# Gate and up projections of an encoder layer: one of the seven Strassen products is itself split by a second Strassen level

## The reference

```python
x = x + 0.5 * swiglu(rmsnorm(x, norm_ffn1), w_ffn1_gate, w_ffn1_up, w_ffn1_down)
x = x + hybrid_mixer(rmsnorm(x, norm_mix), ...)
x = x + 0.5 * swiglu(rmsnorm(x, norm_ffn2), w_ffn2_gate, w_ffn2_up, w_ffn2_down)
y = rmsnorm(x, norm_final)

def swiglu(h, w_gate, w_up, w_down):        # D_FF = 2816
    return (jax.nn.silu(h @ w_gate) * (h @ w_up)) @ w_down
```

## Time and profile before

| | |
|---|---|
| median of 3 runs (lowest to highest) | 2169.91 us (2168.96 to 2171.39) |
| profiled execution, first to last instruction (its span) | 2169.4 us; no time of its own outside the span is listed |
| PE busy | 2138.6 us (99%), 11956 matmuls |
| DVE, ACT, POOL busy | 69%, 39%, 15% |
| moved by DMA | 301.17 MB, 139 GB/s over the span |
| gate and up stages | 34 to 575 us and 1359 to 1900 us of the span |

### The profile page before, as it was taken

How to read it: one execution, slowest core, us unless ns; L and a number is a source line. 1 busy time by engine, 2 the same in 40 slices (tenths; PEclk the granted TensorE clock), 3 DMA queues, 4 the chain that set the end, 5 groups by cost and what they waited for, 6 DMA issues and landing times.

```text
span 2169.4 us, 32769 instructions
## 1 busy us (share of the span) xinstructions
PE 2138.6 (99%) x11956; PEld 1921.3 (89%) x11956; DVE 1499.5 (69%) x2704; ACT 842.6 (39%) x1688; POOL 330.1 (15%) x324
## 2 busy tenths in 40 slices
PE   6999999999999999999999999999999999999998
PEld 6999999999988888888888888899999999988887
DVE  7766677676666686988754556777777667757676
ACT  7333222222343355755543334422323322333343
POOL 7111111111100002201002344211111111100000
PEclk9999999999999999999999999999999999999999
DMA  4322222332586566433355972222322222387554
GB/s 128 101 82 91 92 88 88 97 101 97 176 292 211 174 208 171 126 111 94 94 149 170 292 229 101 65 94 92 115 82 82 92 91 88 113 291 257 174 186 166
DMA packets 245987, 301.17 MB, mean 139 GB/s; under 512 B 24194, under 2 KB 159746, under 8 KB 245828
## 3 DMA queue, kind: packets, MB, share of 16 engines
q1 hardware_dynamic: 237188, 285.97, 41.2%
q10 hardware_dynamic: 8640, 13.11, 1.7%
HBM read 206.29 MB, written 88.47 MB: 136 GB/s over the span
## 4 chain that ended last, share of the span: by engine, by line
PE 95%; DVE 2%; POOL 1%; DMA 1%; issue 1%; ACT 1%; SPq 0%; ACTq 0%; POOLq 0%; DVEq 0%
PE ps L2485 16%; PE ps L2481 12%; PE ps L2483 10%; PE ps L2484 10%; PE ps L2493 8%; PE ps L2495 8%; PE ps L2494 8%; PE ps L2408 4%; PE ps L2410 4%; PE ps L2409 4%; PE ps L2426 2%; PE ps L2428 2%; PE ps L2427 2%; PE ps L2680 1%; PE ps L2654 1%; POOL hs L1121 1%
## 5 line engine op out<-in xcount | busy, mean ns | idle before, releaser
L2485 PE MATMUL ps<-hs,w_lo 128*128 128x384 f32 (+1 forms) x992 | 305.0, 307 | 0.0
L2493 PE MATMUL ps<-w_hi,dh 128*128 128x512 f32 x770 | 300.2, 390 | 0.0
L2495 PE MATMUL ps<-w_hi,dh 128*128 128x512 f32 x770 | 299.7, 389 | 0.0
L1959 DVE TENSOR_TENSOR dh<-dr,dh 128x640 fp32r<-128x640 f32 x154 | 127.2, 826 | 161.4 <-ACT dh L1357 161.2
L2494 PE MATMUL ps<-w_lo,dh 128*128 128x512 f32 x610 | 237.3, 389 | 0.0
L2483 PE MATMUL ps<-hs,w_hi 128*128 128x384 f32 (+1 forms) x644 | 214.4, 333 | 3.4 <-DVE hs L1802 2.6
L1357 ACT CAST dh<-dr 128x640 fp32r<-128x640 f32 x154 | 112.2, 729 | 269.9 <-PE ps L2495 250.1
L2484 PE MATMUL ps<-hs,w_hi 128*128 128x384 f32 (+1 forms) x644 | 213.9, 332 | 0.0
L2481 PE MATMUL ps<-hs,w_hi 128*128 128x512 f32 x588 | 210.2, 391 | 0.0
L2481 PE MATMUL ps<-hs_first,w_hi 128*128 128x512 f32 x588 | 210.2, 391 | 0.0
L2484 PE MATMUL ps<-hq,w_hi 128*128 128x384 f32 x616 | 205.8, 334 | 0.0
(11 more groups left out here) (321 smaller groups left out, 4826.2 us busy)
## 6 DMA issues: line engine op xcount, KB each, us to landing
dr<-hid_mid SPq DMA_DIRECT2D x154, 320.0 KB, 3.2
w_raw<-in_w_ffn_down SPq DMA_DIRECT2D x176, 256.0 KB, 3.6
hid_mid<-st SPq DMA_DIRECT2D x88, 320.0 KB, 4.3
w_raw<-in_w_ffn_gate SPq DMA_DIRECT2D x44, 512.0 KB, 4.1
w_raw<-in_w_ffn_up SPq DMA_DIRECT2D x44, 512.0 KB, 3.9
hid_mid<-sg SPq DMA_DIRECT2D x66, 320.0 KB, 2.2
hq<-o_mid SPq DMA_DIRECT2D x70, 128.0 KB, 3.6
w_raw<-in_w_in SPq DMA_DIRECT2D x14, 512.0 KB, 5.4
```

The lines of the kernel that those rows point to most:

```text
L1959: v.tensor_tensor(a_lo, DR[f][n % D_HID][:, :], a_hi.bitcast(F32), ALU.subtract).then_inc(W["a_lo"], 1)
L2485: last = mm(out, lo[:, k, :], b_hi, start=False, stop=k == 3, skip_group_check=True)
L2493: mm(out, hi, w_h, start=first and p in D_FRESH, stop=False, skip_group_check=True)
L2495: return mm(out, lo, w_h, start=False, stop=last, skip_group_check=True)
```

## The change

In each group, GP2 of the gate unit and GP2 of the up unit share the activations B21. The two weight blocks A12 (gate and up) are put together to a 2x2 matrix (rows: gate, up; columns: two halves of the 512 inputs), and B21 is cut in two halves of inputs and two of tokens. Seven inner products by the same scheme, each 2 slices deep and 320 tokens wide, in three matmuls a slice, replace the two products of 4 slices by 640 tokens. All of them are in the up unit: four new weight blocks L1, LA, LB, LC give seven inner turns (LA one, the others two). A gate unit has now six steps of two turns, an up unit six steps of two turns and the seven inner turns.

The seven split activation operands ("pieces", 640 KB each: high and low, 2 slices, 320 tokens) are made during the first group, used there, and written to DRAM (`inner_mid`); every later group reads all seven back into a ring of three buffers (IN_B). The diff, cut to its core:

```diff
+GU_GATE = (GP1, GP6, GP5, GP7, GP4, GP3)
+L1, LA, LB, LC = range(NP, NP + 4)
+GU_UP = (GP1, L1, GP6, GP5, LA, LB, GP7, GP4, LC, GP3)
+UP_TURNS = ((GP1, 0), (GP1, 1), (L1, 0), (GP6, 0), (GP6, 1), (L1, 1), (GP5, 0), (GP5, 1), (LA, 0), (LB, 0),
+            (GP7, 0), (GP7, 1), (LB, 1), (GP4, 0), (GP4, 1), (LC, 0), (LC, 1), (GP3, 0), (GP3, 1))
+INNER = ((L1, 0), (L1, 1), (LA, 0), (LB, 0), (LB, 1), (LC, 0), (LC, 1))
+INNER_BANKS = (6, 6, 6, 7, 7, 7, 6)
...
+def last_turn(s):
+    return s, 0 if G_ENTRIES[s][1] == LA else 1
+
+def blocks_after():
+    after = {e: [] for e in GORDER}
+    n = 0
+    for s in range(G_RING, G_STEPS):
+        n = max(n, GAT[last_turn(s - G_RING)])
+        after[GORDER[n - 1]].append(s)
+    return after
...
             def load_gu(f, u):
                 q, odd = divmod(u, 2)
                 if u >= RAW and odd:
-                    sp.wait_ge(B["lo"], G_BLOCKS[f] + NP * (q - 1) + last_sum(q - 1) + 1)
+                    sp.wait_ge(*lo_made(f, q - 1, last_sum(q - 1)))
                     sp.wait_ge(B["summed"], 4 * (G_PAIRS * f + q))
...
+            def load_in_b(f, i, m):
+                n = N_INNER * i + m
+                if n < N_INNER + 3:
+                    sp.wait_ge(*inner_pool(f, "b_lo", N_INNER - 1))
+                else:
+                    sp.wait_ge(*done(f, *inner_turn((n - 3) // N_INNER, (n - 3) % N_INNER)))
+                if i == 1:
+                    sp.wait_ge(*piece_stored(f, m))
+                sp.dma_start(IN_B[f][n % 3].bitcast(F32).rearrange("p e k n -> p (e k n)"), inner_mid[f, m]
+                             ).then_inc(in_b_loaded[n % 3], 16)
+
             def gate_up_loads(f):
                 for q in range(1, G_PAIRS):
+                    i = q // 2 - 1
                     load_gu(f, 2 * q + 1)
+                    if q % 2 == 0 and i:
+                        load_in_b(f, i, 3)
                     if q + 1 < G_PAIRS:
                         load_gu(f, 2 * q + 2)
                     if q % 2 and q >= 3:
-                        store_sums(f, q // 2 - 1)
+                        store_sums(f, i)
                     if q % 2 == 0:
-                        store_hidden(f, q // 2 - 1)
+                        if i:
+                            for m in range(4, N_INNER):
+                                load_in_b(f, i, m)
+                        for m in range(3):
+                            load_in_b(f, i + 1, m)
+                        store_hidden(f, i)
+                load_in_b(f, GROUPS - 1, 3)
                 load_down(f, 0)
                 load_down(f, 1)
+                load_in_b(f, GROUPS - 1, 4)
...
+            def inner_sums(f, s):
...
+                if j == GP3 and q % 2 == 0:
+                    v.tensor_tensor(y, x, z, ALU.add).then_inc(L["dve"], 1)
+                if j == LA:
+                    v.tensor_tensor(y, y, a11, ALU.subtract).then_inc(L["dve"], 1)
+                    v.tensor_tensor(x, a11, x, ALU.subtract).then_inc(L["dve"], 1)
+                if j == LB:
+                    v.tensor_tensor(y, a12, y, ALU.subtract).then_inc(L["dve"], 1)
...
+            def inner_step(f, s, c):
+                q, j = G_ENTRIES[s]
+                i, m = q // 2, INNER.index((j, c))
+                pe.wait_ge(B["lo"], G_BLOCKS[f] + s + 1)
+                if i == 0:
+                    pe.wait_ge(*inner_pool(f, "b_lo", m))
+                    b = PIECE[f][m % 2]
+                else:
+                    pe.wait_ge(*in_b_count(f, N_INNER * i + m))
+                    b = IN_B[f][(N_INNER * i + m) % 3]
...
+                if m in INNER_AFTER:
+                    pe.wait_ge(*inner_dve(f, "added", i, INNER_AFTER[m]))
+                hi, lo = g_block(s)
+                out = ps[:, INNER_BANKS[m], 0:QT]
+                for k in range(2):
+                    w = INNER_AT[m] + k
+                    mm(out, hi[:, w, :], b[:, 0, k, :], start=k == 0 and m in INNER_BEGINS, stop=False, skip_group_check=True)
+                    mm(out, hi[:, w, :], b[:, 1, k, :], start=False, stop=False, skip_group_check=True)
+                    last = mm(out, lo[:, w, :], b[:, 0, k, :], start=False, stop=k == 1, skip_group_check=True)
+                last.then_inc(S["done"], 1)
```

More of the change, by code:

```diff
@@ L104, in is_wide @@
+QT = HTOK // 2
 def is_wide(f, s, c):
-    return c == WIDE[f] and s >= NP
+    return c == WIDE[f] and s >= len(GU_GATE) and G_ENTRIES[s][1] < NP
 Z_BANKS, X_BANKS, Y_BANKS = (0, 3), (1, 4), (2, 5)
+INNER_BANKS = (6, 6, 6, 7, 7, 7, 6)
 G_BANKS = (Z_BANKS, X_BANKS, Z_BANKS, X_BANKS, Y_BANKS, X_BANKS, Y_BANKS)
-G_ADDS = (GP6, GP7, GP5, GP4, GP3)
-G_OUT = (GP2, GP5, GP4, GP3)
+G_ADDS = (GP6, GP5, GP7, GP4, GP3)
+G_OUT = (GP7, GP4, GP3)
 G_PAIRS = 2 * GROUPS
-G_STEPS = NP * G_PAIRS
+G_ENTRIES = [(q, j) for q in range(G_PAIRS) for j in (GU_UP if q % 2 else GU_GATE)]
@@ L221, in build, with inner_places @@
         x3 = place(122880, "x3", [P, TT, D_MODEL])
+        def inner_places(f, pieces, sums, in_b, up_c, in_a):
+            return ([place(pieces + 5120 * j, f"piece{f}_{j}", [P, 2, 2, QT], F32R) for j in range(2)],
+                    [place(sums + 2560 * j, f"piece_sum{f}_{j}", [P, 2, HT, P // 2]) for j in range(2)],
+                    [place(x, f"in_b{f}_{j}", [P, 2, 2, QT], F32R) for j, x in enumerate(in_b)],
+                    place(up_c, f"up_c{f}", [P, HTOK]), place(in_a, f"in_a{f}", [P, 6, P]))
+        second = inner_places(1, 17920, 165888, (77312, 159744, 164864), 171520, 82432)
         band = sb("band", [P, 3, P], BF16)
@@ L364, in build @@
         N_TILES = tuple([t + HT * e for t in order for e in range(2)] for order in PAIR_ORDER)
+        H_SLOT = {GP1: 0, GP6: 1, GP7: 2, GP5: 3, GP4: 4, GP3: 5, GP2: 6}
         def h_piece(f, j, e, pair):
+            j = H_SLOT[j]
             if f == 0:
@@ L668, in store_hidden @@
             def store_hidden(f, i):
[L669 to L675, removed]
+                up = 2 * i + 1
+                sp.wait_ge(*gated(f, entry(up, GP7), 1))
+                store_block(f, i, DP4, 3)
+                sp.wait_ge(*gated(f, entry(up, GP4), 1))
+                store_block(f, i, DP2, 1)
+                sp.wait_ge(*inner_pool(f, "mult", i))
+                store_block(f, i, DP1, 0)
             def store_sums(f, i):
@@ new lines, in g_evict @@
+                if j == GP7 and c == 1 and q and q % 2 == 0:
+                    act.wait_ge(hid_stored, 48 * (GROUPS * f + i))
+                    act.wait_ge(hid_summed, 4 * (GROUPS * f + i))
+                    for part in range(2):
+                        act.wait_ge(*bank_kept(f, q, part))
+                    nc.scalar.copy(hid(f, 0), P1[f][:, :]).then_inc(L["act"], 1)
+                if j in G_OUT and q % 2 == 0:
+                    act.wait_ge(*added(f, s, c))
+                    src = {GP7: U3, GP4: P1, GP3: U2}[j][f][:, lo:hi]
+                    out = hid(f, {GP4: 1, GP3: 2, GP7: 3}[j])[:, lo:hi]
+                    nc.scalar.activation(out, src, ACT.Silu).then_inc(S["silu"], 1)
@@ L1832, in g_lo @@
             def g_lo(f, s):
-                q, j = divmod(s, NP)
-                raws = [g_raw(f, q, e) for e in range(2)]
-                src = {GP1: raws[0][:, 0:4, :], GP6: w_sum[1][:, :, :], GP2: raws[0][:, 4:8, :], GP7: raws[0][:, 0:4, :],
-                       GP5: w_sum[0][:, :, :], GP4: raws[1][:, 4:8, :], GP3: w_sum[1][:, :, :]}[j]
+                src, k = g_source(f, s)
                 hi, lo = g_block(s)
@@ L1877, in g_evict @@
                 of, rest = ps[:, G_BANKS[j][c], 0:n], ps[:, G_BANKS[j][c], 512 - n:512]
[L1878 to L1879 removed]
+                if two and j == GP1:
+                    to = p1[:, part]
                     dve.wait_ge(*kept(f, s, c))
```

529 lines of the change are left out of this document (380 added, 149 removed).

## The result

The changed kernel takes 2321.36 us (median of 4 runs, 2319.93 to 2325.8) against 2169.88 us for the kernel before on the same chip: a ratio of 1.0702, 95% interval 1.0689 to 1.0714. It is 7% slower. The direction and the largest cost were as forecast, but the sum of 2236 us was 85 us too low, and the time lies outside the range of 2197 to 2258 us.

A forecast was written before the change was run, and what follows sets the result against it. PE, busy 99% of the span, was taken as the bound: 2169.4 - 19.1 (columns) + 63 (late pieces) + 21.6 (clock) - 1 (start) + 1.5 (piece 6) = 2235.4, with 0.5 to the median 2236 us; range 2197 to 2258.

The forecast's parts named there:

- PE's work: Matmul columns per group: two GP2 steps go, 42 inner matmuls come; 0.87 us gained a group, 19.1 us in 22.
- The fourth piece (m = 3) comes too late: Inner turn (LB, 0): its read queues behind a weight load on SP; 18 waits of 3.5 us, +63 us (47 to 83).
- The clock after such a wait: After most of the 18 piece waits PE runs at half clock; 1.2 us each, +21.6 us (0 to 31).
- In the gate unit GP4 now comes straight behind GP7 ... Cost nothing: Gate unit: DVE adds GP7's first turn while its second runs; no cost with DVE's queue up to 1 us behind.
- DVE's queue becomes the bound as well: Rival: inner turns' adds wait behind low parts, 0.5 to 1 us more a group, 11 to 22 us; chance 0.08.
- Start and first groups: Start and group 0 of each FFN: -1 us for less DVE work, ends -3 and +3; +1.5 for piece 6, ends 0 and 5.
- piece 6: Group 0 of each FFN: made after (LB, 1), up to 1 us late; +1.5 us for both FFNs.

The follow-up runs named there:

- e5: e1 plus GP3 placed between GP7 and GP4 in every gate unit but the first; 2196.05 us, ratio 1.0121.
- e1: Changed kernel with the reads of pieces 3 and 4 issued ahead of the weight load in SP's queue; 2223.81 us, ratio 1.0249.
- e4: Changed kernel with 26 transposes of the identity on PE ahead of the wait at (LB, 0), groups 1 to 9; 2301.13 us, ratio 1.0605.
- e2: Changed kernel with DVE's fourth sum of hidden blocks moved behind the add of (GP7, 0); 2305.69 us, ratio 1.0629.
- e3: Changed kernel with the edits of e1 and e2 together; 2211.6 us, ratio 1.0189.
- e7: e5 with the add of (GP7, 0) inside DVE's starting split, and ACT splitting piece 6 before two weight casts in group 0; 2181.87 us.
- e11: e7 with first-unit turns reordered around GP4, a second-FFN weight block made later and the second piece sum one unit later; 2172.07 us, ratio 1.0011.

## Why the prediction was wrong, by its own steps

**PE's work: right.** The 42 inner matmuls are 0.146 us apart (forecast 0.144), 6.13 us a group (6.07). A group gains 0.81 us in PE's columns in place of 0.87; e5 shows 0.6 to 0.7 of it in the time of a group.

**"The fourth piece (m = 3) comes too late": right.** 18 waits, 63.0 us, in groups 1 to 9 of each FFN and in no other, for the reason given: e1 moves nothing but the place in SP's queue, and they go. Its time came out at 2224 us, where 2227 had been expected of the changed kernel less these waits and their clock.
By the Trainium skill, "DMA: Bandwidth & Descriptors", section "Anatomy of one DMA", which gives the rule for transfers that GpSimd issues, the two would have been in an estimated 4.7 us after the first one's issue. These are SP's, and the trace has 361.3 - 355.48 = 5.8 us; the rows gave 5.5 to 6.2, so they were the better guide.

**"The clock after such a wait": the mechanism right, the term mis-sized.** Forecast were 21.6 us, 1.2 for each wait; the trace has up to 54 in all. In the groups there are 17 falls for the 18 waits, 14 of about 3.4 us and 3 of twice that, and nearly all of this time lies behind the wait, where PE works: 31 us, an estimate from the 1.5 us that one fall costs (neighbouring groups, e4) and the 65 us at half speed. That is the upper end of the step. (The step's own sum is a little low as well: 0.97 over 34 to 36 us is 0.12 us at half clock and not 0.06, which makes 3.4 us.) The rest lies in the starts and groups 0, most of it in 50 to 106 us and 1443 to 1502 us, where waits not foreseen brought falls of their own.
The Trainium skill has the recurring fall, "TensorE: Matmul & The Clock Gate", section "HAM oscillation", and this trace agrees for 17 of the 18 waits.

**"In the gate unit GP4 now comes straight behind GP7 ... Cost nothing": wrong,** and the first failed step. It compared one add of 0.55 us with the 1.39 us of the second turn and allowed DVE 1 us of delay. What stood ahead of the add was never listed: a low part, two sums of weights and a sum of hidden blocks, together 2.9 us, and another low part right before it. It cost 1.2 to 1.5 us in nearly every gate unit from the second group on, 25 us. The rival "DVE's queue becomes the bound as well" had the right engine and nearly the size (11 to 22 us), but another place, the adds of the inner turns, and 0.08 of the chances. It was set at weak because DVE is busy 82%; but a share of busy time says nothing of where in the unit the work lies, and at 81% with another order of turns (e5) the same work cost nothing. The kernel was to be called wrongly foreseen if waits for DVE carried more than 20 us: they carry 42 in these rows.

**"Start and first groups": wrong,** the second failed step and the larger one. +0.5 us were forecast for both FFNs, ends -3 and +8; about 36 were measured, 25 of them PE's waits and most of the others the clock. The same pair GP7, GP4 is in the order of the first five steps, and there DVE has the split of the last pair of tiles ahead of the add: waits of 2.9, 1.8, 7.7 and 4.4 us, each with slow matmuls behind it. The step looked at what the change takes away there (a low part less) and at piece 6, and not at the new order of turns. Piece 6 was up to 3.2 us late in each FFN, not 1.

**The sum by what was measured,** from 2169: in groups 1 to 10 the columns -13, the pieces +63, GP4 behind GP7 +25, the clock +31; the starts and groups 0 +36, their clock with them; and +7 in the groups that no row names, about 0.2 us at each of the 37 waits = 2319, the span after (the terms are rounded). The 85 us that the forecast was short are the 36 of the starts, the 25 of GP4, some 9 of the clock, 6 of columns that did not come, and the 7 (by the spans it is 84).

What stays open: how the last 13 us in the starts and groups 0 divide among DVE, ACT and POOL making seven pieces at once, and what decides whether a given wait brings a fall of the clock. A kernel that keeps the old product in group 0 and uses the second level from group 1 on was not tried; by e5's groups it could be some 13 us faster than the kernel before less what the making of the pieces costs, which is an estimate.

## What to carry to other kernels

When a step moves next to another, write out the whole queue of each engine between the two, with the work that has nothing to do with the change; an engine's share of busy time doesn't tell whether one result is ready in time. A transfer whose operand is needed soon must not stand in the queue behind one that waits for a computation, however idle the DMA engines are. And a saving of 1% per group is lost to one wait of 0.7 us in the group, or to a costlier first group.

## What the runs showed of the hardware

A wait of PE can bring on a fall of its clock to 1.2 GHz, which costs about 1.5 us more. The waits of 3.3 to 4.0 us in the groups brought one 17 of 18 times, of about 3.4 us, in three cases of twice that. It began between 1.0 us before PE was back at work and 1.5 us after. Waits of 1.2 to 1.5 us in otherwise full groups left the clock at 1.00 (e1's group), and the same gap as in the changed kernel, filled with 26 transposes of 128 columns (3.00 us, 0.65 us idle), brought no fall in the group shown and in 15 others.

The length of the wait alone does not decide. One of the 18 waits, 3.45 us up to 253.84, brought no fall. And at the start PE stands 2.93 to 2.94 us before the first turn of GP4, with the same program up to there in the changed kernel and in e1 to e5. A fall came with it in the changed kernel, e1, e2 and e5. None came in e3 and e4, where the matmuls behind it lie 0.17 us apart in place of 0.32, and PE reached its next wait 2.8 us sooner. So two executions of one program can differ by some 3 us for each fall, and steps as small as e7 to e11 have to be read with that in mind.

In the longest wait, 7.7 us up to 1446.6, it began inside (columns as above):

```profile
1442.00:1444.00 2.00, 0.00 (x0) 0.00 (x0) 1.97 (x3) 0.92 (x2) 1.40 (x2) 0.81 0.00 0
1444.00:1446.00 2.00, 0.00 (x0) 0.00 (x0) 1.89 (x4) 0.00 (x0) 1.35 (x1) 0.50 0.00 0
...
1448.00:1450.00 2.00, 2.00 (x11) 2.00 (x10) 0.42 (x1) 0.00 (x0) 0.00 (x0) 0.50 0.00 0
1450.00:1452.00 2.00, 2.00 (x13) 2.00 (x12) 0.00 (x0) 0.06 (x1) 0.00 (x0) 0.99 0.00 0
```

So a long wait is not followed by more slow work than a short one: 3.5 us behind this one, 6.1 us behind the 2.94 us wait up to 51.28. And a wait of 1.81 us at the start, 62.1 to 63.9, was followed by a fall where PE had stood 2.94 us some 12 us earlier; in e3 and e4, without the first fall, it was not:

```profile
64.00:66.00 2.00, 2.00 (x11) 2.00 (x12) 1.77 (x2) 0.24 (x1) 1.08 (x1) 0.56 1.16 329
66.00:68.00 2.00, 2.00 (x9) 2.00 (x9) 1.84 (x3) 0.64 (x2) 0.00 (x0) 0.58 0.49 117
```

A read of 640 KB issued 0.43 us after one of 512 KB landed 5.4 us after its issue, with 380 GB/s moving in all (more loads came behind them), against a median of 4.5 us for the four reads of that size in the earlier trace rows. Moving 101 MB more (402.15 in place of 301.17 MB) cost nothing seen where it was in time: a full group in e5 ran at 190 GB/s with PE never idle.
